# Moving the normalised input of each block to a position of its own in a decoder stack of fp32r matmuls

## Time and profile before

| | |
|---|---|
| median of 3 runs | 995.93 us (992.37 to 1000.08) |
| the profiled execution's own time | 998.9 us |
| its span from first to last instruction | 996.5 us |
| mean granted TensorE clock | 0.994 of full |
| TensorE busy | 960.1 us, 8062 matmuls |
| DVE, ACT, POOL busy | 660.3, 534.8, 186.4 us |
| read from HBM | 170.24 MB |

### The profile page before, as it was taken

How to read it: one execution, slowest core, us unless ns; L and a number is a source line. 1 busy time by engine, 2 the same in 40 slices (tenths; PEclk the granted TensorE clock), 3 DMA queues, 4 the chain that set the end, 5 groups by cost and what they waited for, 6 DMA issues and landing times.

```text
span 996.5 us, 20181 instructions
## 1 busy us (share of the span) xinstructions
PE 960.1 (96%) x8062; PEld 946.0 (95%) x8062; DVE 660.3 (66%) x843; ACT 534.8 (54%) x754; POOL 186.4 (19%) x159
## 2 busy tenths in 40 slices
PE   8999989999999899989999999889999999999995
PEld 7999989999999799989999999889999999999995
DVE  6667586665444877678665444774775779999642
ACT  5566646654444545556655443545554566666541
POOL 2121140000000400149100010455120122222101
PEclk9999999999999999999999999999999999999998
DMA  8533635555555355535655554544443545555521
GB/s 341 191 127 120 218 127 192 191 174 206 173 197 180 112 197 199 179 129 201 211 179 201 207 174 154 205 145 164 139 158 105 178 142 179 200 181 198 210 87 43
DMA packets 25844, 172.17 MB, mean 173 GB/s; under 512 B 3252, under 2 KB 3892, under 8 KB 5432
## 3 DMA queue, kind: packets, MB, share of 16 engines
q1 hardware_dynamic: 25784, 171.30, 49.5%
HBM read 170.24 MB, written 1.05 MB: 172 GB/s over the span
## 4 chain that ended last, share of the span: by engine, by line
PE 63%; DVE 15%; issue 6%; POOL 2%; ACT 2%; DVEq 1%; ACTq 0%; POOLq 0%
PE po L404 19%; PE po L405 19%; PE po L406 19%; DVE wL L1230 7%; DVE xnL L1237 2%; POOL rtok L1806 2%; DVE cval L1741 1%; DVE cgate L1741 1%; DVE apad L1728 1%; ACT wH L790 1%; PE po L432 1%; PE po L433 1%; PE po L431 1%; PE pn L479 1%; PE pc L728 1%
## 5 line engine op out<-in xcount | busy, mean ns | idle before, releaser
L1230 DVE TENSOR_TENSOR wL<-raw,wH 128x1024 fp32r<-128x1024 f32 x318 | 411.7, 1318 | 157.7 <-ACT wH L790 157.3
L790 ACT ACTIVATE wH<-raw 128x1024 fp32r<-128x1024 f32 x318 | 332.3, 1057 | 255.7 <-PE po L406 226.7
L404 PE MATMUL po<-xnH,wH 128*128 128x256 f32 x1376 | 391.4, 284 | 18.9 <-DVE xnL L1237 13.4
L405 PE MATMUL po<-xnL,wH 128*128 128x256 f32 x1376 | 383.6, 279 | 0.0
L406 PE MATMUL po<-xnH,wL 128*128 128x256 f32 x1376 | 383.4, 279 | 0.0
L404 PEld LDWEIGHTS po<-xnH,wH 128*128 128x128 f32 x1376 | 259.2, 188 | 24.3 <-DVE xnL L1237 10.3
L405 PEld LDWEIGHTS po<-xnL,wH 128*128 128x128 f32 x1376 | 260.5, 189 | 0.2
L406 PEld LDWEIGHTS po<-xnH,wL 128*128 128x128 f32 x1376 | 260.0, 189 | 0.0
L404 PE MATMUL po<-hH,wH 128*128 128x256 f32 x688 | 191.4, 278 | 1.3 <-DVE wL L1230 1.3
L405 PE MATMUL po<-hL,wH 128*128 128x256 f32 x688 | 191.3, 278 | 0.0
L406 PE MATMUL po<-hH,wL 128*128 128x256 f32 x688 | 191.3, 278 | 0.0
(11 more groups left out here) (284 smaller groups left out, 1083.8 us busy)
## 6 DMA issues: line engine op xcount, KB each, us to landing
raw<-in_weights SPq DMA_DIRECT2D x158, 1024.0 KB, 4.8
x<-in_xT SPq DMA_DIRECT2D x4, 256.0 KB, 5.7
raw<-in_weights SPq DMA_DIRECT2D x2, 512.0 KB, 5.5
mem<-in_memT SPq DMA_DIRECT2D x1, 1024.0 KB, 13.1
out<-y SPq DMA_DIRECT2D x4, 256.0 KB, 2.4
decayt<-in_decay SPq DMA_DIRECT2D x1, 512.0 KB, 3.7
poolwt<-in_poolw SPq DMA_DIRECT2D x1, 256.0 KB, 3.6
par<-in_params SPq DMA_DIRECT2D x1, 164.0 KB, 3.4
```

The source lines that it names most:

```text
L404: pe.matmul(psum[:, n, 0:T], wH[w][:, wc], aH[:, ac, :], start=start, stop=False)
L405: pe.matmul(psum[:, n, 0:T], wH[w][:, wc], aL[:, ac, :], start=False, stop=False)
L790: act.activation(wH[b % HL][:, hs], raw[b % RAW][:, hs], ACT.Copy).then_inc(s_hi, 1)
L1230: dve.tensor_tensor(wL[b % HL][:, hs], raw[b % RAW][:, hs], wH[b % HL][:, hs].bitcast(f32), ALU.subtract)\
```

## The change

The two tiles xnH and xnL become seven pairs of tiles, one for each gain. All pairs lie in the same room, which is 6 x 64 = 384 bytes larger than before; a pair starts 0, 2, 4, 6, 0, 3 or 2 steps of 64 bytes into it, and its xnL lies directly behind its xnH. Each phase names the pair of its gain. Everything behind the pairs, from memH on, moves by 384 bytes. The pairs share memory; the waits that guarded the single pair are unchanged, and so is every instruction but for its addresses.

```diff
-        xnH = sb("xnH", [P, C, T], f32r)
-        xnL = sb("xnL", [P, C, T], f32r)
+        xn_base, xn_size = place[0], C * T * 4
+        place[0] += 2 * xn_size + 6 * 64
+        xnH, xnL = {}, {}
+        for gain, steps in [("g00", 0), ("g02", 2), ("g10", 4), ("g12", 6), ("gmix", 0), ("gxa", 3), ("gffn", 2)]:
+            first = xn_base + 64 * steps
+            xnH[gain] = sb(f"xnH_{gain}", [P, C, T], f32r, [first])
+            xnL[gain] = sb(f"xnL_{gain}", [P, C, T], f32r, [first + xn_size])
         memH = sb("memH", [P, C, T], f32r)
...
-            phase_slab("qk", 0, xnH, xnL, ready=(s_xn, 0))
+            phase_slab("qk", 0, xnH["g00"], xnL["g00"], ready=(s_xn, 0))
...
+                gain = f"g{layer}2"
...
-                        slab(i * 4 + (s0 + 4 + j), (s0 + j) % HL, slot(g0 + j), xnH, xnL)
+                        slab(i * 4 + (s0 + 4 + j), (s0 + j) % HL, slot(g0 + j), xnH[gain], xnL[gain])
...
-                phase_slab("cin", i, xnH, xnL, ready=(s_xn, 8) if i == 0 else None, between=norm(5) if i == 1 else {})
+                phase_slab("cin", i, xnH["g10"], xnL["g10"], ready=(s_xn, 8) if i == 0 else None, between=norm(5) if i == 1 else {})
...
-                    act.activation(xnH[:, c, :], x[:, c, :], ACT.Identity, scale=col(gain, c)).then_inc(s_xnH, 1)
+                    act.activation(xnH[gain][:, c, :], x[:, c, :], ACT.Identity, scale=col(gain, c)).then_inc(s_xnH, 1)
...
-                    k = dve.scalar_tensor_tensor(xnL[:, c, :], x[:, c, :], col(gain, c), xnH[:, c, :].bitcast(f32),
+                    k = dve.scalar_tensor_tensor(xnL[gain][:, c, :], x[:, c, :], col(gain, c), xnH[gain][:, c, :].bitcast(f32),
                                                  ALU.mult, ALU.subtract)
```

More of the change, by code:

```diff
@@ new lines, in _ @@
+            phase_slab("qk", 1, xnH["g00"], xnL["g00"], between=norm(0) | {6: lambda: gates(0, range(4)), 7: lambda: gates(0, range(4, 8))})
+            phase_slab("qk", 2, xnH["g00"], xnL["g00"], between={0: lambda: gates(1, range(4)), 1: lambda: gates(1, range(4, 8))})
+            phase_slab("qk", 3, xnH["g00"], xnL["g00"], between={6: log_sums})
+            phase_slab("v", 0, xnH["g00"], xnL["g00"], by_token=True, between={1: turn_a})
+            phase_slab("v", 1, xnH["g00"], xnL["g00"], by_token=True, between={2: first_scores, 3: turn_maxima, 7: lambda: scores(1)})
@@ L574, in _ @@
+            phase_slab("v", 2, xnH["g00"], xnL["g00"], by_token=True, between={4: lambda: scores(2)})
+            phase_slab("v", 3, xnH["g00"], xnL["g00"], by_token=True, between={1: lambda: scores(3)})
+            phase_slab("o", 0, xnH["g00"], xnL["g00"], between={0: lambda: numerator(0), 1: lambda: norm_sums(1), 5: lambda: norm_spread(1),
                                                   6: lambda: numerator(1)})
-            phase_slab("o", 1, xnH, xnL, between={1: lambda: turn_head(0), 2: lambda: numerator(2), 6: lambda: turn_head(1),
+            phase_slab("o", 1, xnH["g00"], xnL["g00"], between={1: lambda: turn_head(0), 2: lambda: numerator(2), 6: lambda: turn_head(1),
@@ L576, in _ @@
                                                   7: lambda: numerator(3)})
-            phase_slab("o", 2, xnH, xnL, between={5: lambda: turn_head(2)})
-            phase_slab("o", 3, xnH, xnL, between={7: lambda: turn_head(3)})
+            phase_slab("o", 2, xnH["g00"], xnL["g00"], between={5: lambda: turn_head(2)})
+            phase_slab("o", 3, xnH["g00"], xnL["g00"], between={7: lambda: turn_head(3)})
             def fillers(names, n_norm):
@@ L595, in mlp @@
                 d0 = DRAIN[g0][1]
+                gain = f"g{layer}2"
                 for j in range(4):
-                    phase_slab(up, j, xnH, xnL, ready=(s_xn, 4 * feed) if j == 0 else None,
+                    phase_slab(up, j, xnH[gain], xnL[gain], ready=(s_xn, 4 * feed) if j == 0 else None,
                                between=norm(n_norm) if j == 1 else {})
@@ L680, in _ @@
             for i in range(4):
[L681 to L686, removed]
+                phase_slab("rq", i, xnH["gmix"], xnL["gmix"], ready=(s_xn, 16) if i == 0 else None, between=norm(9) if i == 1 else {})
+            phase_slab("ru", 0, xnH["gmix"], xnL["gmix"])
+            phase_slab("ru", 1, xnH["gmix"], xnL["gmix"], between={4: lambda: ret_scores(0), 6: lambda: ret_scores(1)})
+            phase_slab("rv", 0, xnH["gmix"], xnL["gmix"], by_token=True, between={1: lambda: ret_scores(2), 4: lambda: ret_scores(3)})
+            phase_slab("rv", 1, xnH["gmix"], xnL["gmix"], by_token=True, between={5: lambda: pool_product(0)})
+            phase_slab("rg", 0, xnH["gmix"], xnL["gmix"], between={2: lambda: ret_values(0), 3: lambda: ret_values(1), 4: lambda: ret_values(2),
                                                    5: lambda: ret_values(3)})
-            phase_slab("rg", 1, xnH, xnL, between={0: lambda: pool_product(1), 1: head_squares, 5: lambda: head_spread(0),
+            phase_slab("rg", 1, xnH["gmix"], xnL["gmix"], between={0: lambda: pool_product(1), 1: head_squares, 5: lambda: head_spread(0),
                                                    6: lambda: (head_spread(1), head_spread(2)), 7: lambda: head_spread(3)})
@@ L730, in xa_values @@
                 mm.then_inc(s_xo, 1)
[L732 to L735, removed]
+            phase_slab("wq", 0, xnH["gxa"], xnL["gxa"], ready=(s_xn, 20))
+            phase_slab("wq", 1, xnH["gxa"], xnL["gxa"], between=norm(10))
+            phase_slab("wq", 2, xnH["gxa"], xnL["gxa"], between={0: lambda: xa_scores(0), 2: lambda: xa_scores(1)})
+            phase_slab("wq", 3, xnH["gxa"], xnL["gxa"], between={1: lambda: xa_turn(0), 3: lambda: xa_scores(2), 4: lambda: xa_values(0),
                                                    6: lambda: xa_turn(1)})
@@ L744, in _ @@
             d0 = DRAIN[g0][1]
-            phase_slab("fup", 0, xnH, xnL, ready=(s_xn, 24))
-            phase_slab("fup", 1, xnH, xnL, between=norm(11))
+            phase_slab("fup", 0, xnH["gffn"], xnL["gffn"], ready=(s_xn, 24))
+            phase_slab("fup", 1, xnH["gffn"], xnL["gffn"], between=norm(11))
             with pe.Fori(0, (FT // 2 - 2) // 4) as i:
@@ L749, in _ @@
                     pe.wait_ge(s_drain["V"], i * 4 + (d0 + j))
-                    slab(i * 4 + (s0 + 2 + j), (s0 + j) % HL, slot(g0 + j), xnH, xnL)
+                    slab(i * 4 + (s0 + 2 + j), (s0 + j) % HL, slot(g0 + j), xnH["gffn"], xnL["gffn"])
             s0, g0 = SLAB0["fdown"], GROUP0["fdown"]
```

## The result

The changed kernel takes 1011.21 us (median of 4, 1007.96 to 1013.83) against 998.0 us for the kernel before in the same comparison (median of 4, 992.37 to 1000.76). The ratio is 1.0138, 95% interval 1.009 to 1.0185: slower by 1.4%. In later comparisons the unchanged kernel came out somewhat higher (23 runs on one chip: median 1001.64, 22 of them from 993.78 to 1008.36 and one at 1012.05), and two variants that lie as badly as the changed one had ratios of 1.0102 and 1.0109. So the positions cost some 1.0 to 1.4%, each of the three ratios with an interval of about half a per cent on either side.

A forecast was written before the change was run, and what follows sets the result against it. TensorE, busy for 960 of 996.5 us, was taken to bound the kernel. All three terms were zero, 998.9 + 0, but the median of the runs shown, 996 us, was forecast, range 986 to 1004.

The forecast's parts named there:

- (1): Cost on TensorE of the moved xnH and xnL: zero, bounded by 11.9 us less and 15.8 us more.
- rival B: Position biases the draw to the slow pace, in 452:617, 345:424 and 933:984: 1007.5 us, chance 0.11.
- Where does a pace begin and end? At a pause: TensorE stream: its two paces, 113.3 and 117.8 ns a step, change only at pauses, not when the tile changes.
- All slow: Upper bound in (1): 3550 fast matmuls outside 810:871 turn slow at 4.44 ns each, 15.8 us more, 1014.7.
- all fast: Lower bound in (1): 2684 slow matmuls outside 871:933 turn fast at 4.44 ns each, 11.9 us less, 987.0.
- third: Sign if right: TensorE shows both paces, 113.3 and 117.8 ns, and no other.
- leaving fup out: Stage 810 to 933 is in neither bound because DVE sets it; a pace won saves 0.3 us over five pairs.
- Rival A: Position biases the draw to the fast pace on TensorE: 987.0 us, or 990 if only MLPs and wo obey; chance 0.15.
- Rival C: Position sets a floor below both TensorE paces, 111.8 ns a step: 977 us, chance 0.02.
- (2): Cost on ACT and DVE of xnH writes and xnL operations: zero; bounds 13.4 us cleared or 13.9 us added.
- (3): Everything behind, moved by 384 bytes (y, squares, hH, memk, memv), with its DMAs: zero.
- The scatter: Runs from 992.4 to 1000.1 us fit a pace drawn at each pause, about 5 us; so the median, 996, was forecast.

The follow-up runs named there:

- the sweep of pauses: Matmul-only kernel, bursts of 24, eight input positions, pause before each stretched by 16 to 31 numbers written by DVE; 113.3 to 114 ns in 118 of 143 bursts at 192.
- the first trace: Nothing changed: the profiled execution of the kernel before that the prediction read, every moving tile at 448; 998.9 us.
- the execution at 576: Kernel before with 128 unused bytes ahead of xnH, every moving tile at 576 (distance 64); 1012.82 us, ratio 1.0109.
- At 512: Kernel before with 64 unused bytes ahead of xnH, all moving tiles at 512 (0 modulo 256); 1027.56 us, ratio 1.0299.
- The sweep: Matmul-only kernel without the network, bursts of 48, input tiles at 16 positions 64 bytes apart; 120.0, 117.8, 118.7 and 113.3 ns a step, repeating every 256 bytes.
- the turned round case: Changed kernel with all seven input tiles at 576 (distance 64) and everything behind at 704 (distance 192); 1007.25 us, ratio 1.0039.

## Why the prediction was wrong

**The step that failed is (1), "I take zero, since both paces occur at one and the same position".** The observation was right and the conclusion was not. Two paces at one position show that position is not the only cause; they don't show that it is none. It sets the odds: 118 of 143 bursts at the good pace at distance 192, 13 of 144 at distance 64, none of 96 at 0 and 128 (the sweep of pauses). In place of the zero, the changed kernel ran 2474 more steps slow than the first trace of before, 11.0 us. I had a trace with one position in it for every moving tile, and such a trace can't say what another position does. The forecast should have kept rival B at much more than 0.11 on that ground, above all since the tiles went from one position to five.

**"Where does a pace begin and end? At a pause"** was right for the trace of before, where no tile's change is a change of distance, and wrong as a rule: a change of distance can change it in mid-stream. Inside the MLPs of the changed kernel the pace stayed, as forecast, but there xnH (576, 832) and hH (832) are at the same distance of 64.

**The bounds in (1) were right for two paces, and there are more.** All slow, 1014.7, is within a microsecond of the execution at 576 (1013.9); all fast, 987.0, was never reached. But "at most it turns all of the stream into one pace" meant one of the two that the trace had. At 512 the pace was 120.0 and the time 1027.56, 12.9 us above the bound, and wq's 119.2 in the changed kernel is the "third" that the forecast excluded. One count is off and changes nothing: the long stretches hold 5,311 of the 8062 matmuls, so the rest is 2,751, not some 2,690. The price of 4.44 ns a step, 6.4 us an MLP and the counts are what the account above rests on. The reason for leaving fup out held too: its 1056 steps take 124.1 us at 117.8 throughout (819.09 to 943.23), against 122.9 in the first trace (810.08 to 932.95) with half of them fast. Its share is 1.3 us.

**Rival B is what happened**, with its place (up1 and down1, fdown) and its cause, a worse distance between the two tiles. That it is two streams of reads which then get in each other's way is the reading that fits, as nothing else uses both addresses; no run shows it apart. It was priced at 1007.5 by adding 11.5 us to 996. Added to the 998.9 of the execution whose stretches were counted, that is 1010.4, against 1009.8: of its terms, up1 with down1 (6.4) and fdown (1.9) came, of the 3.1 for cin and out1 only out1's 0.9 (cin's 704 is a good place), and out0 (0.7), out2 (0.8) and fup (1.3) made up for it, less the 0.9 that wo won. That the sum comes so close is in part luck of the draws: another execution of the same kernel took 1007.96. The sweep shows 113.3 to 120.0 ns for moves of 64 bytes. The Trainium skill, "SBUF — State Buffer", "Specifications (TRN2)", names lines of 16 bytes only, by which such a move shouldn't matter; the measurement decides against that. The Trainium skill, "SBUF — State Buffer", "SBUF: two separate sides", has TensorE never wait on anyone. No other engine works during a burst of the sweep, so it says nothing against that as far as other engines go; it shows that the pace of TensorE depends on where its own input and weights lie to each other.

**Rival A** (a bias to the fast pace) has fallen for this change: only cin and wo are at 113.3 of the long stretches. The positions that it left were already at the best distance. **Rival C** (a floor below both paces) has fallen too: the lowest of all distances is 113.3.

**(2) and (3)** held for what they spoke of: xnL 949 to 952 ns in the median against 950, xnH 494 to 504 against 496. Of DMAs, ACT waited for the weights twice, in the first 17 us alone, 2.1 us in all against 1.4 before. But (3) names hH among what moves, and weighs DMAs alone; that TensorE reads hH and mixH too is left to the zero of (1). Those tiles were enough for the whole of the loss: with the inputs at 448 and the rest at 832 it came out at 1011.19.

**The scatter** was read rightly as a draw, with too kind a start: the median of the unchanged kernel is nearer 1001 than 996.

What stays open: why a distance of 192 is the good one and 188 or 196 are not, what in the moment of a restart chooses, and why up0 with down0 drew 117.8 in four of the five traces with its input at distance 192. Beyond the length of the pause, nothing was tried on these.

## What to carry to other kernels

Where matmuls follow each other without a gap and weight loads are about as long as the matmuls, sweep the distance between the stationary and the moving tile modulo 256 bytes in a small kernel before laying out SBUF, and list it again whenever an allocation ahead of either changes; here the one good distance was worth 4 to 6% of a step where the draw fell well, and 1 to 3% of the kernel's time. The good distance is 192 from the stationary to the moving tile, so where a slab swaps the parts, the input belongs at 64 past the weights and not at 192. A change that only enlarges a room moves everything behind it: list the distance of every tile that TensorE reads, before and after. And a trace in which a quantity never varies says nothing about what varying it does.

## What the runs showed of the hardware that was not expected

- With 128x128 fp32r weights loaded for each matmul of 256 columns, the step between matmuls depends on the distance from weight tile to moving tile modulo 256 bytes: 120.0 ns at 0, 117.8 or rarely 113.3 at 64, 118.7 at 128 (120.0 in 8 of 48 bursts of one sweep), 113.3 or 117.8 at 192, and 116.6 to 122.1 at the others tried, but for two bursts of 21 at 16 that took 113.3. It is the distance: moving the weights by 64 bytes moved the classes along.
- At 64 and 192 two paces exist, each stable over long stretches (either for more than 1440 steps of an MLP at 192; 113.3 at distance 64 for some 670 in up0 of the turned round case). A pause some nanoseconds longer or shorter can bring the other, and so can a change of distance in mid-stream.
- With the low tile alone off the good distance, which one matmul in three reads, the mean step is 117.7 ns or more instead of 113.3.
- No distance here came below 113.3 ns for a weight load and 256 columns. The Trainium skill, "TensorE: Matmul & The Clock Gate", "Back-to-back issue gap", has 262 cycles for 256 columns as the gap of a matmul by itself, 109 ns as an estimate at 2.4 GHz.
